# Gated-DeltaNet stage: where the state's query products land, and the order and grouping of the sample group's state decay

## The reference

```python
def step(S, xs):
    u_i, w_i, qk_i, qg_i, kg_i, gl_i = xs
    v_new = u_i - jnp.einsum('bhck,bhkv->bhcv', w_i, S)
    o = jnp.einsum('bhck,bhkv->bhcv', qg_i, S) + jnp.einsum('bhij,bhjv->bhiv', qk_i, v_new)
    S = S * gl_i[..., None, None] + jnp.einsum('bhck,bhcv->bhkv', kg_i, v_new)
    return S, o
S, o = lax.scan(step, s0.astype(F32), (u, w, qk, qg, kg, glast))
```

## Time and profile before

| | us |
|---|---|
| median of 3 runs | 1151.35 |
| lowest and highest run | 1150.45 and 1153.21 |
| profiled execution, its own time | 1150.45 |
| profiled execution, span | 1148.6 |
| PE busy | 995.5 |
| DVE busy | 445.4 |
| ACT busy | 294.4 |
| POOL busy | 266.9 |

### The profile page before, as it was taken

One profiled execution on the slowest core, in us unless ns is written; L12 is line 12 of the kernel. 1 busy time (PEld: TensorE's weight loads), 2 busy tenths in 40 slices (PEclk: granted clock), 3 DMA queues, 4 the chain that ended last, 5 costly groups with the idle time before them and its releaser, 6 DMA issues. The chain is left out here.

```text
span 1148.6 us, 21851 instructions
## 1 busy us (share of the span) xinstructions
PE 995.5 (87%) x8755; PEld 656.0 (57%) x8755; DVE 445.4 (39%) x877; ACT 294.4 (26%) x652; POOL 266.9 (23%) x392
## 2 busy tenths in 40 slices
PE   4899999997999889898799998896599888788866
PEld 1556776775666777887455664354355444444432
DVE  2300000026562365676468862436322222122216
ACT  5100000005552201011367742101023222222222
POOL 6000000321003254500156532000122333333310
PEclk9899999999997999898989998997699888888887
DMA  9995316136400200000464253917499999999945
GB/s 342 358 331 220 147 74 147 44 100 209 161 7 1 42 6 4 3 3 7 106 172 114 69 171 119 340 43 292 147 351 393 392 370 376 359 358 351 382 167 181
DMA packets 86874, 214.09 MB, mean 186 GB/s; under 512 B 31477, under 2 KB 54701, under 8 KB 71086
## 3 DMA queue, kind: packets, MB, share of 16 engines
q1 hardware_dynamic: 73874, 188.93, 47.0%
q0 software_dynamic: 10144, 20.47, 5.7%
q10 hardware_dynamic: 2756, 3.27, 0.8%
HBM read 254.83 MB, written 29.75 MB: 248 GB/s over the span
## 5 line engine op out<-in xcount | busy, mean ns | idle before, releaser
L2173 POOL DMA_INDIRECT ys_dram<-late,ids x49 | 45.4, 926 | 182.8 <-ACT late L2371 178.7
L514 PE MATMUL PS<-hT,wring 128*128 128x288 f32 x256 | 83.5, 408 | 0.0
L515 PE MATMUL PS<-hT,wring 128*128 128x288 f32 x256 | 83.0, 406 | 0.0
L2543 DVE COPY mixT<-PS 128x128 f32<-128x128 f32 x49 | 14.3, 292 | 174.4 <-PE PS L2282 130.1
L2263 PE MATMUL PS<-ring,mixT 128*64 128x256 f32 x304 | 75.0, 403 | 4.4 <-DVE mixT L2529 3.3
L2264 PE MATMUL PS<-ring,mixT 128*64 128x256 f32 x304 | 75.0, 403 | 0.0
L2167 POOL DMA_INDIRECT mixT<-h_dram,ids x49 | 46.7, 952 | 119.1 <-DVE ids L2510 96.4
L2263 PEld LDWEIGHTS PS<-ring,mixT 128*64 128x64 f32 x304 | 44.3, 148 | 37.4 <-issue 16.6
L2197 PE MATMUL PS<-late,mixT 128*128 128x512 f32 x128 | 59.4, 625 | 1.8 <-PEq L2591 1.8
L514 PEld LDWEIGHTS PS<-hT,wring 128*128 128x128 f32 x256 | 48.2, 190 | 16.7 <-issue 2.1
L565 POOL DMA_DIRECT2D late<-in_cache_cmp_k_dram x32 | 17.3, 540 | 171.3 <-issue 171.3
(11 more groups left out here) (540 smaller groups left out, 2260.4 us busy)
## 6 DMA issues: line engine op xcount, KB each, us to landing
ring<-in_expert_w_gate_dram SPq DMA_DIRECT2D x25, 1024.0 KB
ring<-in_expert_w_up_dram SPq DMA_DIRECT2D x25, 1024.0 KB
ring<-in_expert_w_down_dram SPq DMA_DIRECT2D x25, 1024.0 KB
late<-in_w_ada_dram SPq DMA_DIRECT2D x8, 2048.0 KB
late<-in_expert_w_gate_dram SPq DMA_DIRECT2D x8, 1024.0 KB
late<-in_expert_w_up_dram SPq DMA_DIRECT2D x8, 1024.0 KB
late<-in_expert_w_down_dram SPq DMA_DIRECT2D x8, 1024.0 KB
mod_r<-in_expert_w_gate_dram SPq DMA_DIRECT2D x8, 1024.0 KB
```

What stands on the lines that cost most here:

```text
L514: MM(PS[:, b, 0:HALF], lhs, hT[:, k, 0:HALF], **s)
L515: last = MM(PS[:, b + 1, 0:HALF], lhs, hT[:, k, HALF:NTOK], **s)
L2173: pool.indirect_dma_start(m.ys_dram.ap(), bass.IndirectOffsetOnAxis(ap=ids[:, 1, j:j + 1], axis=0), yr[:, n % 2, :], None, bounds_check=LA ...
```

## The change

Three things are changed.

1. The query products of a chunk, and with them the qk products and ACT's copy, use the partitions of half c of bank 6, the same half as the w products, where they used the other half. The four query products no longer alternate with the four w products: they come behind them. `ws_ps` is counted between the two. The wait for ACT's copy lies ahead of the query products only, and asks for the copy of chunk n-1 where it asked for that of chunk n-2.
2. `Sn` lies in the values' half of `m.kvt`, tiles 0 to 3, where it lay in `m.yT`. So POOL waits for `wu_ps` at 4 ahead of it.
3. The eight POOL instructions of 64x512 become two of 64x2048. DVE waits once for both.

```diff
-        Sn = m.yT[:, M4:2 * M4, 0:NB * HD].rearrange("p m (b v) -> p m b v", b=NB)
+        Sn = m.kvt[:, 0:M4, W:2 * W].rearrange("p m (b v) -> p m b v", b=NB)
...
             pool.wait_ge(ss_in, 32)
+            pool.wait_ge(wu_ps, PT)
             pool.wait_ge(qg_ok, TILES)
-            for mm in range(M4):
-                for e in range(2):
-                    if mm or e:
-                        pool.wait_ge(sn_ok, 2 * mm + e)
-                    G_.tensor_tensor(Sn[half[e], mm], Ss[half[e], :, mm], egls[half[e], :, 2 * mm + e].unsqueeze(2).to_broadcast([HD, NB, HD]), ALU.mult).then_inc(sn_ok, 1)
+            for e in range(2):
+                if e:
+                    pool.wait_ge(sn_ok, 1)
+                G_.tensor_tensor(Sn[half[e]], Ss[half[e]].rearrange("p b m v -> p m b v"),
+                                 egls[half[e], :, e::2].rearrange("p b m -> p m b").unsqueeze(3).to_broadcast([HD, M4, NB, HD]), ALU.mult).then_inc(sn_ok, 1)
...
-                nc.scalar.copy(o(i)[half[c], :], PS[half[1 - c], 6, :]).then_inc(o_ok, 1)
+                nc.scalar.copy(o(i)[half[c], :], PS[half[c], 6, :]).then_inc(o_ok, 1)
...
+            dve.wait_ge(sn_ok, 2)
             for mm in range(M4):
-                dve.wait_ge(sn_ok, 2 * mm + 2)
                 dve.wait_ge(su_ps, mm + 1)
...
-                pe.wait_ge(qg_ok, i + 1)
-                if n >= 2:
-                    pe.wait_ge(o_ok, n - 1)
                 for mm in range(M4):
                     last = MM(PS[half[c], 7, col(mm)], wT[:, i % 2, c, mm, :], pair(mm), start=True, stop=True)
-                    MM(PS[half[1 - c], 6, col(mm)], m.yT[:, mm, i * P + c * C:i * P + (c + 1) * C], pair(mm), start=(mm == 0), stop=False, skip_group_check=True)
                 last.then_inc(ws_ps, 1)
+                pe.wait_ge(qg_ok, i + 1)
+                if n:
+                    pe.wait_ge(o_ok, n)
+                for mm in range(M4):
+                    MM(PS[half[c], 6, col(mm)], m.yT[:, mm, i * P + c * C:i * P + (c + 1) * C], pair(mm), start=(mm == 0), stop=False, skip_group_check=True)
...
-                    last = MM(PS[half[1 - c], 6, head(e, mm)], qk[half[c], i, blk(e, mm)], vf[half[c], head(e, mm)],
+                    last = MM(PS[half[c], 6, head(e, mm)], qk[half[c], i, blk(e, mm)], vf[half[c], head(e, mm)],
```

## The result

The kernel became slower: a median of 1167.38 us over 4 runs (1164.31 to 1172.31) against 1152.03 us before (1150.45 to 1153.21), ratio 1.0115, 95% interval 1.0079 to 1.0151. This ratio is not the quotient of the two medians, which is 1.0133: the record holds 21 executions of the changed kernel, from 1160.30 to 1172.31 us, with a median of 1165.38. In a second series the changed kernel took 1166.25 us (5 runs) against 1152.63 us over 29 runs, ratio 1.0129 (1.0102 to 1.0156). The direction was forecast. The size was not: both medians lie above the forecast of 1161 us and above its range, 1155.5 to 1163.5.

A forecast was written before the change was run, and what follows sets the result against it. PE is busy 87% of the span; PE's list bounds entries 8 to 10, DVE's entry 12. Terms 3.2 + 4.45 + 2.3 = +9.9 us on 1150.45, plus 0.9 to the median, forecast 1161 us, range 1155.5 to 1163.5.

The forecast's parts named there:

- Term 1: Delta stage chunks: w and query products in one half queue, 0.86 us more PE time per chunk; +3.2 us in sum.
- what moves back is `level_t`, by 0.86 us: PE's list per chunk: `ws_ps` comes no earlier, and `level_t` starts 0.86 us later because the products queue.
- The new wait for ACT: Query products of chunk n wait for the copy of chunk n-1; tightest at chunk 3 with 0.45 us to spare; cost 0.
- Term 2: Entry 12: POOL's two long instructions, 3.64 us each, hold DVE instructions with two SBUF inputs; +4.45 us.
- Term 3: Behind entry 12: PE idles 5.3 us, so the granted clock falls to 0.50; +2.3 us, between 1.7 and 2.9.
- Rivals A: Behind entry 12 the clock doesn't fall; only queueing and POOL's hold count, +7.7 us, 1159 us; chance 0.13.
- B: POOL doesn't hold DVE for a whole long instruction, or starts elsewhere; +3.2 to +4.1 us, 1154.6 to 1155.4; chance 0.11.
- C: The array halves did not work side by side, so queueing costs nothing; sum +5.9 us, 1157.3 us; chance 0.07.
- what the delta stage gains or loses moves everything behind it by the same amount: Stages behind the delta stage: nothing there started early enough to hide its change, so all of it reaches the total.
- Rival D: Behind the delta stage: a later start re-lays the clock's low stretches, making the kernel faster, 1148.8 us; chance 0.07.

The follow-up runs named there:

- the order alone: Kernel before with query products placed behind the w products, still in the other half of bank 6, POOL as before: 1154.78 us against 1152.63, ratio 1.0018.
- the half alone: Kernel before with query products, qk products and ACT's copy in half c, alternating order and POOL as before: 1159.37 us against 1153.08, ratio 1.0047.

## Why the prediction was right or wrong

- **Term 1, the queueing.** The mechanism was right, and its measure in entry 8 (1.89 instead of 1.03 us) too. The size was off: 4.42 us measured for 3.2. Of the 1.2 missing, 0.31, 0.24 and 0.31 are in chunks 1 to 3. The step that failed is "what moves back is `level_t`, by 0.86 us": it looked at the query products alone. The qk products write the same half as well, and their overlap with the end of the key products and with the second `level_t` shrinks. The run with the order alone keeps the other half and does not have this part, and the run with the half alone has all of the 1.17 us. The other 0.4 is chunk 5, where the sum said +0.1 and 0.50 came; with the order alone it is 0 there, so it hangs on the half too, but which wait lets it through was not looked at. Chunk 6 was right (0.55 and 0.48), and so were chunks 0, 4 and 7.
- **The new wait for ACT**: 0, as forecast. In the changed kernel L1460 follows L1454 without a gap in entry 10.
- **Term 2, POOL**: 4.66 measured, 4.45 forecast, from 3.68 and 4.01 us per instruction. The forecast's 3.64 us and its 0.33 us of hold on the second (4.01 against 3.68 where POOL runs alone) both came. The port rule of the Trainium skill's page "SBUF — State Buffer", section "SBUF: two separate sides", holds for long instructions too: 0.28 us behind POOL's end in both kernels. The 4497 ns of the Trainium skill's page "GPSIMD Engine Reference", section "3.1 Elementwise — side-by-side cycle accounting", lies above the 3.68 and 4.01 us measured for the same count; the measurement decides.
- **Term 3, the clock**: 1.97 in one profile and 3.6 in another, 2.3 forecast with 1.7 to 2.9. It fell at about 527.3, where 521.5 plus the shift of some 5.7 us was expected. The fall was rightly forecast, and it came in all four profiles with this wait and no fillers. Its reason was weaker than the text says: the wait of 2.99 us that it was taken from left the clock at 1.00 in 5 of 18 profiles.
- **The sum of the stage**: 4.42 + 4.66 + 1.97 = 11.05, and 63.11 - 52.07 = 11.04. With -0.08 in entry 7 and -0.46 behind chunk 7 it is the 10.5 of the profiles, for 9.9 forecast. Rivals A, B and C all fall: the clock did fall, POOL did hold DVE for the whole instruction, and the halves had worked side by side.
- **The step that failed for the total** is "what the delta stage gains or loses moves everything behind it by the same amount", together with the base that it was added to. The stage grew by 10.51 us, close to the 9.9 of the sum, but in the first pair of profiles the attention stage grew by 6.0 us more and the part ahead of chunk 0 by 2.1, at the same code. Rival D named a mechanism of this kind, low stretches of the clock behind the stage that change, with the wrong sign. What the runs show in place of the step is that these parts differ from one execution to the next by as much as the change is worth: the low stretch near the start of the attention stage lasts 7 us in one profile of the kernel before and 31 in the other, 27 in one of the changed kernel and 7 in the other. The base was one execution of before with the short one, and a median of 1151.35 us over 3 runs, where later series of 29 to 35 runs gave 1152.6 to 1154.8. The range took no account of this spread: its bounds were those of POOL and of one stretch of the clock (they add up to 1163.2 at the top), with nothing for the stages around.
- **What stays open.** The two series without fillers give +15.4 and +13.6 us between medians, with intervals that reach down to 1.008 and 1.010. All executions on record, 26 of the changed kernel and 140 of the kernel before, have means of 1165.6 and 1153.7, 11.9 us apart; two series of the kernel before differ by 2.0 us in their means, so this is no sharper. The part from chunk 0 to the attention stage took 105.9 to 109.0 us in the changed kernel and 95.4 to 96.8 in the kernel before (three profiles each, one of them with attention fillers): 9.1 to 13.6 us more. That the delta stage is most of the cost is shown; whether the change adds anything outside it is not. Of the 13 profiles without attention fillers the long stretch stands in four of the six in which `Sn` lies in `m.kvt`, and in one of the seven others, which is too few to tell a cause from chance. What decides between 7 and 31 us within one kernel was not found.

## What to carry to other kernels

Look at the half of the array that each small product writes before its order: two products that write different halves cost the time of one, in alternation and partly even when they stand apart, and a gain from that is lost for every later product that shares the half. Fewer and longer GpSimd instructions are only better where VectorE has no instruction with two SBUF inputs to run; place them where VectorE waits for something else. Take the time and the granted clock of each stage over several executions before forecasting a total: here the attention stage took 142.6 and 150.1 us in two profiles of the same kernel.

## What the runs showed of the hardware

- Products on different halves can start out of the order of the list, by the starts in the trace: with eight w instructions ahead of them, the query instructions began after the fifth, at 491.29, and the sixth w instruction followed at 491.40.
- A VectorE instruction with two SBUF inputs ended 0.28 us behind the end of the GpSimd instruction that it met, for GpSimd instructions of 1.06 and of 4.01 us (the larger one of 128x512 ended 0.54 us behind).
- The same wait of TensorE, 2.99 us at the same place, was followed by the clock at 0.50 in 13 profiles and by 1.00 in 5. And a low stretch can last although TensorE has work: it was busy for 26.00 of 26 us at 0.50.
- Four filler matmuls, 3.4 us of added PE work in places where PE idled 0.2 to 1.3 us, made the kernel 0.41% faster (interval 0.12% to 0.70%). In the five profiles with them the long stretch of the attention stage was absent.
